# The block-wise inverse of an RWKV-7 stage on 64x64 tiles, its passes written out, four tiles moved to 128-byte starts

## The reference, cut to what matters

```
def rwkv7_step(state, inp):
    r, w, k, v, a, b = inp
    sa = jnp.einsum('bhvk,bhk->bhv', state, a)
    state = state * w[:, :, None, :] + sa[..., None] * b[:, :, None, :] + v[..., None] * k[:, :, None, :]
    y = jnp.einsum('bhvk,bhk->bhv', state, r)
    return state, y
```

```
        h = rmsnorm(x, norm_mix_pre[l])
        proj = h @ w_in[l]
        ...
        merged = (g_a * (y_a @ wb[:RWKV_WIDTH])
                  + g_b * (y_b @ wb[RWKV_WIDTH:RWKV_WIDTH + CONV_WIDTH])
                  + g_c * (y_c @ wb[RWKV_WIDTH + CONV_WIDTH:]))
        x = x + rmsnorm(merged @ w_out[l], norm_mix_post[l])
        h = rmsnorm(x, norm_ffn_pre[l])
        gate, up = jnp.split(h @ w_ffn_in[l], 2, axis=-1)
        x = x + rmsnorm((jax.nn.silu(gate) * up) @ w_ffn_out[l], norm_ffn_post[l])
```

## Time and profile before

| | before |
|---|---|
| median of 3 runs | 1185.17 us (1179.21 to 1185.38) |
| the profiled execution's own time | 1180.94 us |
| its span, first to last instruction | 1179.2 us |
| TensorE matmuls, busy | 1086.3 us, 92% |
| TensorE weight loads, busy | 891.3 us, 76% |
| VectorE / ScalarE / GpSimd, busy | 42% / 32% / 38% |
| mean granted TensorE clock | 0.959 |

### The profile page before, as it was taken

The page is one execution under the profiler, slowest core; times in us unless marked ns, Lnnn a source line. Parts: engine busy times, 40 slices in busy tenths (PEclk is TensorE's granted clock), DMA queues, the critical chain, the costliest instruction groups (busy, mean ns, idle before and its releaser), DMA issues.

```text
span 1179.2 us, 13967 instructions
## 1 busy us (share of the span) xinstructions
PE 1086.3 (92%) x5541; PEld 891.3 (76%) x5541; DVE 489.9 (42%) x579; ACT 376.7 (32%) x483; POOL 446.4 (38%) x339
## 2 busy tenths in 40 slices
PE   3998999999989998999868999977999999999997
PEld 2886788778867886787756577766888888888885
DVE  4014662775277437735835656243222222210003
ACT  5111512341244124312265153254323322321112
POOL 6445321541154225422410125405455445444431
PEclk8999899999999999999969899987999999999999
DMA  6232321241133113341710245512333332332221
GB/s 214 72 107 71 107 90 54 72 139 58 54 110 111 64 53 107 107 170 52 277 36 1 89 143 178 214 36 72 107 85 93 107 102 76 106 107 84 95 72 72
DMA packets 106751, 116.93 MB, mean 99 GB/s; under 512 B 2462, under 2 KB 86492, under 8 KB 106716
## 3 DMA queue, kind: packets, MB, share of 16 engines
q1 hardware_dynamic: 98080, 99.10, 26.1%
q10 hardware_dynamic: 8636, 17.34, 3.8%
HBM read 100.17 MB, written 16.25 MB: 99 GB/s over the span
## 4 chain that ended last, share of the span: by engine, by line
PE 61%; issue 15%; DVE 14%; POOL 5%; ACT 4%; ACTq 1%; DMA 0%; DVEq 0%; POOLq 0%
PE ps L1191 13%; PE ps L1192 13%; PE ps L1193 13%; PE ps L1281 10%; POOL w_lo L524 5%; PE ps L1338 3%; PE ps L1331 3%; DVE sq L915 1%; DVE xm L894 1%; DVE xm L895 1%; PE ps L1316 1%; PE ps L1359 1%; PE ps L1366 1%; DVE xm L893 1%; DVE h_f L833 1%
## 5 line engine op out<-in xcount | busy, mean ns | idle before, releaser
L524 POOL TENSOR_TENSOR w_lo<-w_raw,w_hi 128x512 fp32r<-128x512 f32 x304 | 435.7, 1464 | 702.7 <-ACT w_hi L556 702.7
L556 ACT CAST w_hi<-w_raw 128x2048 fp32r<-128x2048 f32 x76 | 145.0, 1908 | 209.4 <-PE ps L1193 181.0
L1191 PE MATMUL ps<-a_hi,w_hi 128*128 128x512 f32 x512 | 201.5, 394 | 7.6 <-issue 3.8
L1192 PE MATMUL ps<-a_lo,w_hi 128*128 128x512 f32 x512 | 200.9, 392 | 0.0
L1193 PE MATMUL ps<-a_hi,w_lo 128*128 128x512 f32 x512 | 200.9, 392 | 0.0
L1281 PE MATMUL ps<-a_hi,w_hi 128*128 128x512 f32 x384 | 158.8, 414 | 0.0
L1281 PE MATMUL ps<-a_lo,w_hi 128*128 128x512 f32 x384 | 152.7, 398 | 0.0
L1281 PE MATMUL ps<-a_hi,w_lo 128*128 128x512 f32 x384 | 152.0, 396 | 0.0
L1191 PEld LDWEIGHTS ps<-a_hi,w_hi 128*128 128x128 f32 x512 | 97.3, 190 | 28.6 <-issue 8.3
L1193 PEld LDWEIGHTS ps<-a_hi,w_lo 128*128 128x128 f32 x512 | 97.1, 190 | 20.5
L1192 PEld LDWEIGHTS ps<-a_lo,w_hi 128*128 128x128 f32 x512 | 97.3, 190 | 20.1
(11 more groups left out here) (247 smaller groups left out, 1486.7 us busy)
## 6 DMA issues: line engine op xcount, KB each, us to landing
w_raw<-w_in SPq DMA_DIRECT2D x34, 1024.0 KB, 5.2
w_raw<-w_ffn_in SPq DMA_DIRECT2D x44, 512.0 KB, 4.9
spill<-spill_buf ACTq DMA_DIRECT2D x27, 512.0 KB, 2.8
w_raw<-w_ffn_out SPq DMA_DIRECT2D x11, 1024.0 KB, 4.8
w_raw<-w_branch SPq DMA_DIRECT2D x5, 1024.0 KB, 8.8
proj<-spill SPq DMA_DIRECT2D x1, 4608.0 KB, 15.9
g_ab<-spill SPq DMA_DIRECT2D x8, 512.0 KB, 5.1
w_raw<-w_out SPq DMA_DIRECT2D x4, 1024.0 KB, 5.3
```

The costliest lines, as they stand in the source:

```text
L524: last = g.tensor_tensor(w_lo[:, b, c], w_raw[:, b, c], w_hi[:, b, c].bitcast(F), ALU.subtract)
L556: s.copy(w_hi[:, b], w_raw[:, b]).then_inc(hi_ready, 1)
L1191: t_.matmul(dst, w0, a0, start=first, stop=False)
L1192: t_.matmul(dst, w0, a1, start=False, stop=False)
```

## The change

- The tiles tt and wt become [128, 8, 64] and qb [128, 8, 32]: chunk 0 of each head on partitions 0 to 63, chunk 1 on 64 to 127 (the sides are named half). mab goes away: mt's block 2 - half is the matrix itself. The memset of mab at the start of the recurrence goes with it.
- Each of Q, T and the final turn is 16 matmuls of 64x64 weights in place of 8 of 128x128. They are issued in the order TILES, on alternating partition halves: (head 0, half 0), (head 4, half 1), (head 1, half 0), ... The two of a neighbouring pair write different PSUM banks. Q and T move 32 columns in place of 64; the final turn is an ordinary fp32 matmul with an identity and moves 64.
- VectorE's operations in the levels have half the elements. The transposition ahead of level 0 is two of 64 partitions.
- The low-rank matmuls of L1294 and L1297 alternate between the halves, and so do those of L1316, which now wait for mt_ready before head 4 and no longer before head 5.
- The four passes of rwkv are written out on VectorE, ScalarE and TensorE.
- The arena starts at a multiple of 128 bytes, and y_hi too; y_lo, f_hi and f_lo follow.
- GpSimd makes the level masks in a temporary and copies half of them and two identities of 64x64: four more small copies, ahead of its first work on weights.

```diff
-        top = [(nc.sbuf_base + 63) // 64 * 64]
+        top = [(nc.sbuf_base + 127) // 128 * 128]
...
-        ARENA = top[0]
+        ARENA = (top[0] + 127) // 128 * 128
...
-        mab, o = arena("mab", [P, NH, P], o)
-        wt, _ = arena("wt", [P, NH, P], o)
+        wt, _ = arena("wt", [P, NH, HD], o)
-        tt, _ = arena("tt", [P, NH, P], e)
+        tt, _ = arena("tt", [P, NH, HD], e)
-        qb, _ = arena("qb", [P, NH, HD], o)
+        qb, _ = arena("qb", [P, NH, HD // 2], o)
...
-        y_hi, o = arena("y_hi", [P, BT, SEQ], AT_C, R)
+        y_hi, o = arena("y_hi", [P, BT, SEQ], (AT_C + 127) // 128 * 128, R)
...
+        TILES = [((i + NH // 2 * half) % NH, half) for i in range(NH) for half in range(2)]
...
-            link(v.memset(mab[:], 0.0))
...
-                    for c in range(2):
-                        r = other[c]
-                        v.tensor_tensor(mab[r, hs, r], m_ps[r, :, 1 + c],
-                                        causal_chunk[r, 1:2].broadcast_to((HD, 2, HD)), ALU.mult)
...
-                link(v.transpose(wt[:], mab[:]))
+                for half in range(2):
+                    last = v.transpose(wt[own[half]], mt[own[half], :, 2 - half])
+                link(last)
...
+                def part(bank, h, half):
+                    return ps[own[half], bank + 2 * (h // 4), h % 4 * (HD // 2):(h % 4 + 1) * (HD // 2)]
...
-                    t_.matmul(ps[:, 0, c], lora_up[0:HD, c], xm[0:HD, RT - 2], start=True, stop=True)
-                for j in range(NJ):
-                    c = slice(j * P, (j + 1) * P)
-                    last = t_.matmul(ps[:, 1, c], lora_up[HD:P, c], xm[HD:P, RT - 2], start=True, stop=True)
+                    for half in range(2):
+                        last = t_.matmul(ps[:, half, c], lora_up[own[half], c], xm[own[half], RT - 2], start=True, stop=True)
...
-                    for h in range(NH):
-                        rhs = tt[:, h].rearrange("p (n two b) -> p n two b", two=2, b=1 << lv)[:, :, 0]
-                        last = t_.matmul(ps[:, 0, h * HD:(h + 1) * HD].rearrange("p (n b) -> p n b", b=1 << lv), mab[:, h], rhs,
+                    for h, half in TILES:
+                        rhs = tt[own[half], h].rearrange("p (n two b) -> p n two b", two=2, b=1 << lv)[:, :, 0]
+                        last = t_.matmul(part(0, h, half).rearrange("p (n b) -> p n b", b=1 << lv), mt[own[half], h, 2 - half], rhs,
                                          start=True, stop=True)
...
-                    for h in range(NH):
-                        last = t_.matmul(ps[:, 1, h * HD:(h + 1) * HD], wt[:, h], qb[:, h], start=True, stop=True)
+                    for h, half in TILES:
+                        last = t_.matmul(part(1, h, half), wt[own[half], h], qb[own[half], h], start=True, stop=True)
...
-                for h in range(NH):
-                    last = t_.transpose(ps[:, 3 + h // 4, h % 4 * P:(h % 4 + 1) * P], tt[:, h], ident[:])
+                for h, half in TILES:
+                    last = t_.matmul(ps[own[half], 3 + h // 4, h % 4 * HD:(h % 4 + 1) * HD], tt[own[half], h],
+                                     ident[own[half], own[half]], start=True, stop=True)
...
-            passes(pe, rwkv, NT)
+            for T in range(NT):
+                rwkv(T)
```

More of the change, by code:

```diff
@@ L73, in hybrid_layer @@
     PER_T = 6
+    LO_PARTS = 4
     S_REST = N_RWKV + NT * PER_T
@@ L119, in hybrid_layer @@
         head_rows = nc.alloc_sbuf_tensor_at("head_rows", [P, 2 * P], F, offset=top[0])
[L120 removed]
+        level_mask = fixed("level_mask", [P, LEVELS, HD // 2])
+        ident_pair = fixed("ident_pair", [P, HD])
         head_ones = fixed("head_ones", [P, P])
@@ L484, in _ @@
             pool.wait_ge(ident_ready, 1)
-            link(g.memset(level_mask[:], 1.0))
+            link(g.memset(wide_mask[:], 1.0))
             link(g.memset(causal[:], 1.0))
@@ L512, in _ @@
                 link(g.tensor_copy(causal_chunk[r, 0::3], causal[r, 1:2, r].broadcast_to((HD, 2, HD))))
-                last = g.tensor_copy(causal_chunk[r, 1:3], causal[r, 0:1, r].broadcast_to((HD, 2, HD)))
+                link(g.tensor_copy(causal_chunk[r, 1:3], causal[r, 0:1, r].broadcast_to((HD, 2, HD))))
+                link(g.tensor_copy(ident_pair[r], ident[r, r]))
+                last = g.tensor_copy(level_mask[r], wide_mask[r, :, HD // 2 * half:HD // 2 * (half + 1)])
                 if half == 0:
@@ L624, in evacuate @@
                         act.wait_ge(first_tile, T * PER_T + (k + 1))
-                        if not (isinstance(T, int) and k < 2):
+                        if not (T == 0 and k < 2):
                             act.wait_ge(spilled[b], T * (8 * PER_T) + 16 * (k // 2))
@@ L960, in rwkv @@
                         need(q_ready, 0)
-                        add = qb[:].rearrange("p h (n b) -> p h n b", b=1)
+                        hn = "p h n b -> p (h n) b"
+                        add = qb[:].rearrange("p h (n b) -> p h n b", b=1).rearrange(hn)
+                        dst = dst.rearrange(hn)
                     else:
                         need(t_done, lv - 1)
-                        add = ps[:, 1].rearrange("p (h n b) -> p h n b", h=NH, b=1 << lv)
-                    hn = "p h n b -> p (h n) b"
-                    v.tensor_tensor(dst.rearrange(hn), dst.rearrange(hn), add.rearrange(hn), ALU.add).then_inc(t_ready.sem, 1)
+                        add = ps[:, 1:4:2, 0:P].rearrange("p a (m b) -> p a m b", b=1 << lv)
+                        dst = dst.rearrange("p (a h) n b -> p a (h n) b", a=2)
+                    v.tensor_tensor(dst, dst, add, ALU.add).then_inc(t_ready.sem, 1)
                     if lv < LEVELS - 1:
@@ L1009, in rwkv_pass @@
                 rwkv(T)
-            passes(dve, rwkv_pass, NT)
+            for T in range(NT):
+                rwkv_pass(T)
             ch.end(NT)
@@ L1276, in fill_steps @@
                             pe.wait_ge(lo_ready, T * PER_T + (N_RWKV + k + 1))
-                        if kt == 0 and step == 0 and not (isinstance(T, int) and q < 2):
+                        if kt == 0 and step == 0 and not (T == 0 and q < 2):
                             pe.wait_ge(spill_copied, T * (2 * PER_T) + (q - 1))
@@ L1308, in rwkv @@
                 last.then_inc(toks_done.sem, 1)
-                for h in range(NH):
-                    if h == 1:
-                        need(g_ready)
-                    if h == 5:
+                need(g_ready)
+                for j in range(NJ):
+                    if j == 2:
                         need(mt_ready, 0)
                     for c in range(2):
[L1315 to L1319, removed]
+                        for h in (2 * j, 2 * j + 1):
+                            col = j % 2 * 2 * P + c * P
+                            last = t_.matmul(ps[:, mt_bank(h), col:col + P], heads(bkd, h)[:, c * P:(c + 1) * P],
+                                             heads(ar, h)[:, c * P:(c + 1) * P], start=True, stop=True)
+                            if c == 1 and j % 2:
+                                last.then_inc(mt_done.sem, 1)
                 fill(4)
@@ L1350, in rwkv @@
                         need(s_ready, c - 1)
-                    elif not isinstance(T, int):
+                    elif T > 0:
                         pe.wait_ge(s_ready.sem, T * 2)
@@ L1365, in rwkv @@
                     for h in range(NH):
-                        last = t_.matmul(ps[ru, 1, h * HD:(h + 1) * HD], wt[ru, h, ru], xs[ru, h], start=True, stop=True)
+                        last = t_.matmul(ps[ru, 1, h * HD:(h + 1) * HD], wt[ru, h], xs[ru, h], start=True, stop=True)
                     last.then_inc(u_done.sem, 1)
```

23 lines of the change are left out of this document (12 added, 11 removed).

## The result

| | before | after |
|---|---|---|
| median of 4 runs, same chip | 1182.88 us (1179.21 to 1185.38) | 1148.7 us (1148.4 to 1149.15) |
| ratio, 95% interval | | 0.9718 [0.9699, 0.9736] |
| the profiled execution's own time | 1180.94 us | 1148.54 us |
| its span | 1179.2 us | 1146.6 us |
| mean granted TensorE clock | 0.959 | 0.966 |

A forecast was written before the change was run, and what follows sets the result against it. TensorE's issue time was taken as the bound. Terms -23.2 + 1.6 - 1.8 - 1.6 - 0.9 - 4.8 = -30.7 us gave 1150.2 from the profiled 1180.94; the forecast, set between this and the run median, was 1152 us, range 1143 to 1178.

The forecast's parts named there:

- What bounds the kernel: Whole kernel, including the recurrence: TensorE's own issue time sets the length, so a saving on TensorE saves kernel time.
- that rival: Levels: sparser 64x64 groups let the granted clock fall to 1.2 GHz; 5 us a pass would give 1170; chance 0.04.
- Two halves side by side: Q, T, final turn: 32 alternating instructions take 1.74 us a group; levels -23.2 us, turn +1.6; chance 0.62.
- the near end: Group time of Q and T: 1.74 us, halves overlapping, taken over the other bound, 2.68 us one after the other.
- in part: Rival, Q, T and turn: halves overlap only halfway, a group is 2.21 us, kernel 1170.9 us; chance 0.17.
- not fed so fast: Rival, the 44 groups: 0.059 us issue per instruction with load, 2.68 us a group, kernel 1191.6 us; chance 0.12.
- The 128-byte starts: High products of merge and w_ffn_out: tiles starting at multiples of 128 save 6.3 ns an instruction, -4.8 us.
- The rival that the place is not the cause: High products with y_hi and f_hi: tile place does not cause the 6.3 ns; 4.8 us less gain, 1155.0; chance 0.06.
- Passes written out: Turn of the recurrence's loop: writing the four passes out was priced at 0.
- Low-rank matmuls: L1294 to L1299: strict alternation takes 1.19 us instead of 1.64, 0.45 a pass, -1.8 us; bound: nothing.
- Products of L1316: Second part, waiting for mt: without mab, mt starts 0.52 us earlier; 0.4 us a pass, -1.6 us; bounds 0 and -2.1.
- Memset of mab: VectorE, between last projection and xm: removing it saves 0.9 us, once.

The follow-up runs named there:

- Two lines more: The changed kernel with fixed tiles and arena at multiples of 256 bytes instead of 128: 1143.81 us, ratio to before 0.9694; again on another chip 1146.0 us, 0.9693.
- The undone order: The changed kernel with the low-rank matmuls and L1316's products back in their old order: 1151.85 us, ratio to before 0.9758.

## Why the prediction was right, and where not

**What bounds the kernel: right.** Levels off TensorE's time came out one to one. The clock stayed at 1.00 in pass 1, so that rival falls, and TensorE waits for VectorE in no level.

**Two halves side by side: right.** 1.71 us measured for 1.74 forecast, which is the gain of the levels (-23.5 for -23.2) and of the turn's cost (+1.3 for +1.6). Some -1.0 of the levels' gain belongs to the passes written out: the forecast read T as 2.40 us in pass 1, inside the loop, where pass 0 has 2.32. The choice of the near end rested on one pair of equal starts in the earlier trace rows; the run with one half after the other shows that it was the right mechanism. Both the rival "in part" and the one "not fed so fast" needed 2.21 us or more. The second is refuted by the record of 32 instructions in 1.12 us: 29 ns for a load and a matmul. Pairs of instructions of one tile in succession, the worry of the first, cost nothing that shows, and two tiles in succession only 0.02 us a group. That moving 32 or 64 columns makes no difference also holds: 1.12 and 1.15 us a record.

**The 128-byte starts: wrong.** The failed step is "**-4.8 us**, if the place is the cause". The 6.3 ns were real and the place does decide them, but not as a multiple of 128: alone the edits give a ratio of 0.9993. What counts is whether moving and stationary tile agree by 256, and the four kinds of operands in the earlier trace rows can't tell these apart, since w and a share a remainder and f and y had two others. The rival that the place is not the cause had the right time for this term and the wrong reason. Two lines more give the missing part: 119.0 us in place of 122.0 in w_ffn_out, and some 1.4 in the merge by its steps. The medians, 1143.8 us for 1148.7, say the same less sharply, since they are from two chips; beside the kernel before, the ratios are 0.9694 and 0.9718, and their intervals overlap.

**Passes written out: wrong.** The failed step is "I price it at 0. The turn of the loop has no row of its own". The trace had one, on VectorE and not on TensorE: 0.68 us of idleness between two instructions of VectorE, and behind it stands the wait for xm of the earlier trace rows. Alone the edit gives -3.5 us, 0.9965 [0.9952, 0.9977].

**The sum: near by luck.** Place of the tiles, 5.2 us too little in the last stretches, was offset by terms that the forecast had at nothing or too small: 2.2 from the passes written out (without the 1.0 that the levels already hold), 2.5 in attention, 1.1 at the start and 0.9 in the low-rank matmuls.

**Low-rank matmuls: right mechanism, size off.** -2.7 for -1.8. In passes 1 to 3 alternation took 1.09 us and not 1.19; in pass 0, where the clock is low (0.50 before, 0.59 after), 2.01 for 3.02. The undone order confirms 2.7.

**Products of L1316: right**, -1.6, by mab's absence alone. **Memset of mab: right.** The first xm comes 2.0 us earlier, of which 0.6 is an earlier first dense product (25.46 us, 26.09 before). From that product to the first xm it is 82.2 us before and 80.9 after; over all traces, the three with the memset have 81.4 to 82.2 and the nine without 79.8 to 81.3, and the means are 0.9 apart, as forecast. The rest of the 2.0 is no more than one execution differs from the next.

**Left over.** The attention section, from y's last transposes to the first product of the merge, is 2.5 us shorter (118.4 us for 120.9) with unchanged code. That is variation from execution to execution: the kernel with all at multiples of 256, profiled twice, has 121.0 and 118.4, and the kernel before with the address edits alone has 118.5. It belongs to no part of the change.

## What to carry to other kernels

The small fp32 matmuls here are bound by their loads of weights, which go by columns (0.115 us an instruction with 128 columns, 0.058 with 64). Splitting a block-diagonal 128x128 tile into two 64x64 tiles on different partition halves halves the time of the instructions only if the halves alternate at least every four of them. When operands of the same matmul form show different steady times, compare the addresses of the two operands with each other before rounding one of them. When TensorE's work gets shorter, look at what waits it now has and move the independent work to them: here that was worth another 12.9 us. A gap at a loop's turn on another engine can be the head of such a wait. And one trace holds microseconds that belong to the execution: a second profile of the same kernel tells which.

## What the runs showed that I had not expected

- An fp32r matmul of 512 columns starts every 226.7 ns when moving and stationary tile have equal remainders by 256 bytes, and every 232.4 to 233.3 when not (remainders 128 and 32 apart; 64 apart is slow too, by its median of 394 ns for 389); 128 and 128 is as good as 0 and 0.
- TensorE sustains 32 alternating 64x64 fp32 instructions, loads included, at 29 ns each; in a row on one half they are some 58 apart.
- The look-ahead that makes two halves overlap is short, three instructions: bunches of 4 instructions cost 0.02 us a group of 32, of 8 0.31, of 16 0.72.
- The turn of this hardware loop leaves VectorE idle for 0.65 to 0.68 us, its entry from the written-out pass 0.36, and T on TensorE takes 0.07 us more in each looped pass than in a written-out one.
